# Down projections of two feed-forward layers as token rows, by seven block products in place of eight

## The reference, cut to what matters

```python
def squared_relu_mlp(h, w_up, w_down):          # (512, 1024), (1024, 4096), (4096, 1024)
    return jnp.square(jax.nn.relu(h @ w_up)) @ w_down

for i in range(DEPTH):                          # DEPTH = 2
    ...                                         # mixer and cross-attention
    h = h + squared_relu_mlp(rms_norm(h, norm_ffn[i]), ffn_w_up[i], ffn_w_down[i])
return rms_norm(h, norm_final)
```

## Time and profile before

| | |
|---|---|
| median of three runs | 1913.2 us |
| profiled execution, span | 1909.6 us |
| TensorE busy | 1857.5 us, 97% |
| VectorE busy | 1052.6 us, 55% |
| ScalarE busy | 747.2 us, 39% |
| GpSimd busy | 168.8 us, 9% |
| mean granted TensorE clock | 0.996 of full speed |

### The profile page before, as it was taken

One profiled execution on the slowest core, in us unless ns is written; L12 is line 12 of the kernel. 1 busy time (PEld: TensorE's weight loads), 2 busy tenths in 40 slices (PEclk: granted clock), 3 DMA queues, 4 the chain that ended last, 5 costly groups with the idle time before them and its releaser, 6 DMA issues.

```text
span 1909.6 us, 38661 instructions
## 1 busy us (share of the span) xinstructions
PE 1857.5 (97%) x17053; PEld 1527.4 (80%) x17053; DVE 1052.6 (55%) x1405; ACT 747.2 (39%) x999; POOL 168.8 (9%) x135
## 2 busy tenths in 40 slices
PE   6999999999999999999999999999999999999997
PEld 5898658778888888785779999998787788888886
DVE  4897655444432442447659888887654344324422
ACT  4434664334422332223544434343643343213322
POOL 1000002000000000210013111111020010000000
PEclk9999999999999999999999999999999999999999
DMA  6226223213332232453442112112362123332221
GB/s 215 89 71 233 78 100 133 66 45 93 106 111 88 89 111 88 137 159 127 154 147 62 51 50 53 49 31 70 126 217 70 44 89 102 97 110 89 88 88 44
DMA packets 165503, 189.41 MB, mean 99 GB/s; under 512 B 11801, under 2 KB 152646, under 8 KB 163674
## 3 DMA queue, kind: packets, MB, share of 16 engines
q1 hardware_dynamic: 162016, 174.44, 28.8%
q0 software_dynamic: 3088, 12.45, 1.7%
q10 hardware_dynamic: 234, 0.06, 0.0%
HBM read 161.22 MB, written 21.51 MB: 96 GB/s over the span
## 4 chain that ended last, share of the span: by engine, by line
PE 51%; DVE 3%; ACT 2%; issue 1%; DMA 1%; ACTq 0%; DVEq 0%
PE ps L357 11%; PE ps L358 10%; PE ps L359 10%; PE ps L2372 7%; PE ps L2338 2%; PE ps L2385 1%; PE ps L2326 1%; PE ps L1706 1%; PE ps L2349 1%; PE ps L1313 1%; PE ps L1746 1%; PE ps L2468 1%; ACT weights_split L326 1%; PE ps L2305 1%; PE ps L1294 1%
## 5 line engine op out<-in xcount | busy, mean ns | idle before, releaser
L344 DVE TENSOR_TENSOR weights_split<-w,weights_split 128x2048 fp32r<-128x2048 f32 x117 | 268.1, 2291 | 243.1 <-ACT weights_split L326 238.2
L326 ACT ACTIVATE weights_split<-w 128x2048 fp32r<-128x2048 f32 x118 | 225.9, 1914 | 285.7 <-PE ps L359 265.9
L357 PE MATMUL ps<-x_hn_hi,weights_split 128*128 128x512 f32 x640 | 252.7, 395 | 0.0
L359 PE MATMUL ps<-x_hn_hi,weights_split 128*128 128x512 f32 x640 | 249.2, 389 | 0.0
L358 PE MATMUL ps<-x_hn_lo,weights_split 128*128 128x512 f32 x640 | 249.0, 389 | 0.0
L357 PE MATMUL ps<-f_hidden_hi,weights_split 128*128 128x512 f32 x512 | 199.3, 389 | 0.0
L359 PE MATMUL ps<-f_hidden_hi,weights_split 128*128 128x512 f32 x512 | 199.2, 389 | 0.0
L358 PE MATMUL ps<-f_hidden_lo,weights_split 128*128 128x512 f32 x512 | 199.2, 389 | 0.0
L1565 DVE SCALAR_TENSOR_TENSOR f_relu<-ps,x_squares 128x512 f32<-128x512 f32 x64 | 44.1, 692 | 191.1 <-PE ps L359 172.5
L358 PEld LDWEIGHTS ps<-x_hn_lo,weights_split 128*128 128x128 f32 x640 | 120.2, 188 | 26.3 <-issue 1.4
L357 PEld LDWEIGHTS ps<-x_hn_hi,weights_split 128*128 128x128 f32 x640 | 120.1, 188 | 26.2 <-issue 1.4
(11 more groups left out here) (365 smaller groups left out, 3464.0 us busy)
## 6 DMA issues: line engine op xcount, KB each, us to landing
w<-in_ffn_w_up_dram SPq DMA_DIRECT2D x32, 1024.0 KB, 5.4
w<-in_ffn_w_down_dram SPq DMA_DIRECT2D x32, 1024.0 KB, 5.0
w<-in_xattn_w_kv_dram SPq DMA_DIRECT2D x15, 1024.0 KB, 5.4
w<-in_ab_w_in_dram SPq DMA_DIRECT2D x10, 1024.0 KB, 5.1
w<-in_xattn_w_q_dram SPq DMA_DIRECT2D x8, 1024.0 KB, 5.0
w<-in_xattn_w_o_dram SPq DMA_DIRECT2D x8, 1024.0 KB, 4.9
w<-in_ab_w_out_dram SPq DMA_DIRECT2D x4, 1024.0 KB, 5.5
w<-in_rwkv_w_r_dram SPq DMA_DIRECT2D x4, 1024.0 KB, 5.9
```

The costliest lines, as they stand in the source:

```text
L326: act.activation(hi, raw, ACT.Copy).then_inc(k.w_hi_ready, 1)
L344: eng.tensor_tensor(lo, raw, hi.bitcast(F32), ALU.subtract).then_inc(k.w_lo_ready, 1)
L357: pe.matmul(out, lhs[0], rhs[0], start=start, stop=False)
L359: return pe.matmul(out, lhs[1], rhs[0], start=False, stop=stop)
```

## The change

Only the down projections, the hidden chunks that they read, and what comes after them change; the products with `w_up` stay as they are.

**Seven products.** The 4096 hidden units go in four quarters of 1024. In a quarter the down projection is a product of a 2 x 2 block matrix of hidden values (token halves by halves of the hidden units) with a 2 x 2 block matrix of weights (512 rows by 512 columns). It is computed with seven block products in place of eight, each for 256 tokens by 512 output columns: P1, P2, P5, P6, P3, P7, P4 in this order, each 24 matmuls of 512 columns (4 chunks of rows, 2 token tiles, 3 of `mm3`). The hidden values are now the stationary operand, the weights the moving one, and outputs are token rows.

**Hidden blocks.** Two chunks (one slot of `w_up`) give seven 128 x 256 pieces for the seven products: four squares and three sums. `tm` holds eight pieces and is used once at a time. Of the first chunk, VectorE makes the relu (L1642), ScalarE squares it in place (L1523), VectorE subtracts (L1704), ScalarE rounds two pieces (L1526), VectorE takes their remainder (L1652); of the second chunk the same with three sums (L1708 to L1710, each waiting for the former), five pieces to be rounded and left over.

**Weight sums.** A quarter has 4 slots of `w_up` and 4 raw slots of `w_down`, and 11 splits: four, three raw blocks, and four sums. `combine` (VectorE, L397) makes a sum in place, a subtraction of 128 x 2048. A fourth weight buffer (`f_weights`) is added in the feed-forward.

**Output.** VectorE takes each product's two tiles from PSUM and adds them to the sums `down_sums_left` and `f_down_sums_right` (128 tokens x 512 each, L1664 to L1678). In layer 0 the sums are transposed back at the end, 32 transposes, and added to `h`, and only then are the eight chunks squared and the squares added on GpSimd. In layer 1 `h` is transposed into the sums during the first quarter (ScalarE copies them), and at the end each row tile is squared with its row sum on ScalarE, the root taken by Sqrt and reciprocal, and the rows scaled in place and stored.

The diff, cut to its core:

```diff
@@ weights, Kernel.plan_weights
-            for half in range(0, FF, FF // 2):
-                cols(f"up{l}", i["ffn_w_up"][l], half, half + FF // 2)
...
+            for r in range(0, FF, D):
+                cols(f"up{l}", i["ffn_w_up"][l], r, r + D)
+                rows = i["ffn_w_down"][l][r:r + D, :].rearrange("(j k p) c -> k p j c", k=2, p=P)
+                for b, n in ((0, 1), (1, 1), (0, 0), (1, 0)):
+                    self.slots.append((f"down{l}", [(None, None, rows[b, :, :, n * D // 2:(n + 1) * D // 2])]))
...
+                    x12, x22, x11, x21 = range(s - 3, s + 1)
+                    n = len(self.units)
+                    self.units += [(x11, 0), (x21, 0), (x11, sums + 1), (x11, sums + 3), (x22, 0), (x12, sums + 2),
+                                   (x21, sums + 4)]
+                    sums += 4
+                    for x in (x12, x22):
+                        self.release[x] = (self.w_lo_ready, n + 6)
+                    self.release[x11] = (self.w_sums, sums)
+                    self.release[x21] = (self.w_lo_ready, n + 7)
@@ Split
+    def combine(self, dve, i, a, b):
...
+        dve.wait_ge(k.w_lo_ready, k.rested)
...
+        dve.tensor_tensor(flat(s), flat(sa), flat(sb), ALU.subtract).then_inc(k.w_sums, 1)
@@ stage_layer, TensorE
+            def down(q):
+                for x, (name, part, bank, u, half, right) in enumerate(PRODUCTS):
+                    ws.wait(pe, WF + NS * q + 4 + u)
...
+                        if by_row and m == 0:
+                            pe.wait_ge(s_hlo, 2 * (y0 + 4 * q + j) + x + 1)
+                        mm = mm3(pe, outs[m], [h[:, j, part, m * P:(m + 1) * P] for h in hid],
+                                 ws.wide_pair(WF + NS * q + 4 + u, j), j == 0 and name in ("P1", "P2", "P5"), j == 3,
+                                 bank is not None)
...
+                for n, c in enumerate(TURN):
...
+                        m = pe.transpose(k.bank(turned[n])[:, t * P:(t + 1) * P],
+                                         sums[c // 4][:, t, c % 4 * P:(c % 4 + 1) * P], k.ident)
+                    m.then_inc(k.done(turned[n]), 1)
                 squares[2].sum(pe)
@@ stage_layer, ScalarE
+                    for m in range(2):
+                        k.wait_freed(act, up[q][2 * a + m])
+                        r = tm[:, 3 * m:3 * m + 2, :]
+                        act.activation(r, r, ACT.Square).then_inc(s_hsq, 1)
+                        act.wait_ge(s_hcomb, 2 * y + m + 1)
+                        b = slice(3, 8) if m else slice(1, 3)
+                        act.activation(hid[0][:, a, b.start - 1:b.stop - 1, :], tm[:, b, :], ACT.Copy).then_inc(s_hhi, 1)
...
+                    ws.round(act, WF + NS * q + a + 2)
+                for x in range(7):
+                    ws.round(act, WF + NS * q + 4 + x + 2)
@@ stage_layer, VectorE
+                    relu(q, a, 0)
+                    dve.wait_ge(s_hsq, 2 * y + 1)
+                    dve.tensor_tensor(tm[:, 2, :], tm[:, 1, :], tm[:, 0, :], ALU.subtract).then_inc(s_hcomb, 1)
+                    remainder(q, a, 0)
+                    relu(q, a, 1)
+                    dve.wait_ge(s_hsq, 2 * y + 2)
+                    k.dve.link(dve, dve.tensor_tensor(tm[:, 5, :], tm[:, 0, :], tm[:, 3, :], ALU.add))
+                    k.dve.link(dve, dve.tensor_tensor(tm[:, 6, :], tm[:, 5, :], tm[:, 1, :], ALU.subtract))
+                    dve.tensor_tensor(tm[:, 7, :], tm[:, 4, :], tm[:, 6, :], ALU.subtract).then_inc(s_hcomb, 1)
+                    ws.rest(dve, W + a + 2)
+                    remainder(q, a, 1)
+                    if a == 2:
+                        ws.combine(dve, U + 2, U + 5, U)
+                    elif a == 3:
+                        ws.combine(dve, U + 5, U + 4, U + 5)
+                for x in range(7):
+                    if last and q == 3 and x == 6:
+                        break
+                    take(q, x)
+                    ws.rest(dve, U + x + 2)
+                    if x == 0:
+                        ws.combine(dve, U + 3, U + 4, U + 2)
+                    elif x == 1:
+                        ws.combine(dve, U + 6, U + 1, U + 3)
+                    if last and q == 3 and x == 4:
+                        dve.wait_ge(s_out, 16)
+                        for t in (2, 3):
+                            mean(t, t + 1)
+                        for t in (2, 3):
+                            root(t, t + 3)
+                            scaled(t, 0)
+                            scaled(t, 1)
```

More of the change, by code:

```diff
@@ L296, in __init__ @@
         self.k, self.base = k, k.splits
-        assert k.to_split[self.base] == s0, "slots are split in order"
+        assert k.units[self.base][0] == s0, "slots are split in order"
         k.splits += len(ends)
@@ L424, in mm_chunks @@
             o, t = tok
[L425 removed]
+            m = pe.matmul(k.bank(n)[:, o:o + width], src[:, c, t:t + P], k.raw(slot)[:, c, col:col + width],
                           start=(c == 0), stop=(c == 7))
@@ L1361, in _ @@
+            for q in range(4):
+                for a in range(4):
+                    i = WF + NS * q + a
+                    if q == a == 0:
+                        mm3_first(pe, k, up[0][0], ws, b_pair.both, lambda c: hf.wait(pe, c), WF)
+                        squares[1].sum(pe)
+                    else:
                         ws.wait(pe, i)
                         for m in range(2):
-                            n = down[half] + 2 * a + m
-                            if d == 0:
-                                k.take(pe, n)
```

439 lines of the change are left out of this document (252 added, 187 removed).

## The result

| | before | after |
|---|---|---|
| median of 4 runs each, us | 1912.53 (1911.54 to 1913.42) | 2007.11 (2005.48 to 2008.23) |
| profiled span, us | 1909.6 | 2006.1 |
| mean granted TensorE clock | 0.996 | 0.969 |

The ratio is 1.0494, with a 95% interval of 1.0479 to 1.0509: the changed kernel is 4.9% slower. The forecast was 2005 us.

What follows compares the result with a forecast made beforehand. TensorE bounds the old kernel; the changed one was to wait on the serial VectorE and ScalarE chain. 39.6 + 44.0 + 10.4 - 1.8 = +92.2 us gives a span of 2001.8, plus 3.6: 2005 us, range 1980 to 2032.

Steps and rivals of the forecast that it cites:

- a slot's chain: Serial VectorE and ScalarE work per slot of w_up: 12.65 us, 14.86 with a weight sum, where TensorE needs 10.88; chance 82%.
- differences of 256: VectorE's subtractions for the hidden sums, not in the earlier trace: 0.42 us each, bounds 0.27 and 0.68.
- Hand-overs: Passing work between engines: 0.04 us each, eleven per slot; 0.10 each would give 2025 us, inside the main case.
- A quarter's waits: TensorE waits 1.4 us before P1, 2.7 before its last row chunk, 6.7 before P2, then 1.6, 1.2 and 0.3.
- the signs named: Expected in the changed profile: TensorE share some 91%, named waits, quarters of 95.5 us, over 8 us idle between layers.
- The clock: Rival: TensorE's half clock after the wait before P2 falls on the path, +14 us, 2019 us; chance 6%.
- The rival of late weights: At quarter changes, weight slots share bandwidth and the first lands 2 us late: +12 us, 2017 us; chance 6%.
- The end of layer 0: Last product to the next stage's matmuls: squares, six GpSimd adds, sum with ones 1.3, entry 1.0; +10.4 us.
- The end of layer 1: Tail after P4 shorter by 7 us, P4 waiting 5.2 us for P7's bank: net -1.8 us.
- The turned copies: In layer 1's first quarter ScalarE copies two transposed chunks per slot ahead of the rounding: +4.4 us.
- The stages between: From the stage after layer 0 to layer 1's first relu: forecast change 0.
- The time around the span: Median above the profiled span by 3.6 us, added to the forecast span of 2001.8 us.

Runs made afterwards that it cites:

- round_early: The changed kernel with ScalarE rounding the next slot's weights right behind the second chunk's square, ahead of the copy of 1280: 1931.35 us.
- remainder_first: The changed kernel with VectorE taking the remainder of 1280 before the next slot's split remainder, in place of behind it: 1968.2 us.
- clock_held: The changed kernel with 26 extra TensorE matmuls before the wait for P2's weights, to keep its clock up: 2007.81 us.
- sums_moved: The changed kernel with two weight sums moved, from slot 3 to behind P2 and from behind P2 to behind P5: 1998.53 us.
- scaling_later: The changed kernel with VectorE, in layer 1's last quarter, taking P7's tiles before scaling the first two row tiles: 2004.75 us.
- all_orders: The changed kernel with early rounding, moved sums, later scaling, and GpSimd adding only four squares after layer 0, TensorE summing the rest: 1908.07 us.

## Why the prediction was right

**The bound.** It said that TensorE would stop being the bound because a slot's chain on the two other engines lasts longer than TensorE's 10.88 us. The slots of 12.59 and 14.81 us show it, and round_early and remainder_first show that it is the order, not VectorE's load: the same instructions in two other orders ended at 10.87 (TensorE's own time; the chain there is 9.93) and 11.20 us a slot.

**The durations.** The two sizes that were not in the trace came out as the slope of the others said: differences of 256 in 0.42 to 0.43 (0.42), the remainder of 1280 in 1.48 (1.49), the copy of 1280 in 1.27 (1.27). Hand-overs: relu 565.92 + 0.68 to its square at 566.64 is 0.04. The value of the earlier trace rows was the right end of the bound and the 0.10 of the earlier trace rows the wrong one; had it been 0.10 at each of the eight changes of engine in a slot, 12.65 would have become 13.1. (The prediction counts eleven; the order of a slot has eight, and two waits of VectorE for itself.)

**A quarter's waits.** Forecast 1.4, 2.7 and 6.7; the trace has 0.83, 2.34 and 5.14. Add the 0.27 that goes unrecorded at each wait and they are 1.1, 2.6 and 5.4. The last is short by 1.3 because the six matmuls ahead of it ran at the half clock, 6 x 0.20 = 1.2 us longer, and P2's start is set by VectorE: 53.66 against 54.05. Behind P2 the forecast had waits of 1.6, 1.2 and 0.3 us; the trace has none before P5 and 0.1 to 0.2 before P6 and P3, because P2's slow matmuls filled the time. P6 started 13.8 us behind P2's start, where 13.9 was forecast. Of the signs named, two came out a little off: TensorE's share is 93% and not 91%, as slow matmuls count as busy, and its wait for GpSimd's adds 7.9 us and not over 8.

**The clock.** The prediction gave 6% to a loss on the path of 14 us, and held that P2's would be covered: 5.69 + 1.7 = 7.4 us against VectorE's 7.30. It was covered, as clock_held shows, but by another sum. P2 took 8.2 us, and P5's split was ready after 7.0; the 1.2 us between were hidden by the wait before P6, with 0.1 us to spare. That it held is in part luck, and in sums_moved it held no longer. In two places there was no cover, and the clock was in no term: the sum with ones at the end of layer 0 (1.9 us of its 3.8) and P4 at the end (7.5 for 5.44). Together 4.0 us; these are the step that failed, a term left out: both follow a wait that the prediction itself had worked out (over 8 us, and 5.2 us), and the earlier trace rows had shown what comes after one. I had carried that to P2 alone. Nor had the clock fallen only once in the kernel before: it is 0.50 from 235 to 238 us too, behind idle times of 0.41 and 0.80 us.

**The weights.** The rival of late weights has nothing for it. The slots of `w_up` landed later after their issue than before (medians 7.4 us into `w` and 8.7 into `f_weights`, 5.4 before), but in neither feed-forward did TensorE, VectorE or ScalarE wait for a transfer.

**The end of layer 0** was +12.4 for +10.4: the add chain right to 0.1 us, the sum with ones 2.5 over, of which 1.9 are the clock and 0.6 a term sized too low, and the entry to the next stage 0.5 in place of 1.0. **The end of layer 1** was forecast at -1.8 with P4's wait and the shorter tail; both were right to 0.3 us. P4's slow 2 us does not show in the layer's sum (+41.7 for +42.2) since two other sizes were off the other way, which is luck. The turned copies cost 3.9 and not 4.4: the first quarter took 93.1 us in layer 0 (457.88 to 550.98) and 97.0 in layer 1 (1614.17 to 1711.15). And before, layer 1 took 336.2 us from its first relu to its last product (1559.35 to 1895.56) against layer 0's 334.4, which I had taken as equal. 39.5 + 3.9 - 1.8 for the quarters, and for the end 5.35 + 2.06 - 7.3: 41.7.

**The stages between** were taken as unchanged; their gaps of "issue" grew by 3.1 us, and the stages by 3.0. The gaps were 11.8 in scaling_later's profile with the same instructions there, so part of this differs from execution to execution. What makes them stays open.

**The time around the span** was taken as 3.6 us, the median of before less the profiled span. The executions themselves show 1.8 us (2007.89 for a span of 2006.1), the rest was the distance between two executions. The forecast's 2005 thus came out 2.1 below 2007.11 with a span 4.3 below 2006.1; with the 1.8 it would have been 2003.6. A part of its closeness is luck.

**The expectations** were a little lower than the result, by 2 to 5 us, the largest in all_orders (1903 for 1908.07); only clock_held's range held the result. Each assumed that nothing but the named step would wait, and sums_moved's left out the clock.

## What to carry to other kernels

Before taking work off the engine that is the bound, add up for one stage of the loop the chain on the engines that feed it, with each one's order and with every tile that exists once, and compare it with the bound engine's new time for that stage; mean busy shares (55% and 39% here) say nothing on it. If the chain is longer, look for the in-order engine whose next independent instruction stands behind a wait: one such instruction moved ahead of its wait was worth 76 of 95 us. And wherever the sum has a long idle time of TensorE, ask whether what stands behind it is on the path, and then cost its first microseconds at the half clock. What hides that loss is often the same wait that one would like to remove: in sums_moved the second quarter gained nothing, since P2's slow matmuls came out from under it.

## What the runs showed of the hardware that was not expected

- The half clock came after shorter waits than the one of 4.42 us in the earlier trace rows. In the changed kernel the matmuls of 596.57 lie 0.43 us apart behind an idle time of 2.34 us, with one of 0.83 us at 589.86 ahead of it, and those behind the 0.83 alone lie 0.23 apart.
- The same idle times are not always followed by it. In sums_moved's fourth quarter waits of 0.83 and 2.33 us stand ahead of the matmuls of 784.88, and these lie 0.23 us apart at a granted clock of 1.00. And it can come late: behind 3.18 us of idle time the matmuls of the changed kernel from 469.21 on start at the full clock, and only from 470.63 on, over a microsecond later, do they lie 0.43 apart.
- P4's matmuls were slow for about 4 us behind 5.35 us of idle time (1991.88 to 1995.86), P2's for about 5.3 (604.64 to 609.93) behind 5.14, and in the last quarter for only 2.7 behind 5.69 (1955.68 to 1958.41).
- A square that also sums its row is followed by a read of the accumulator, an instruction of its own: the read starts 0.54 us behind the square, the next square 0.76.

```profile
1984.65 0.64 ACT L1550 ACTIVATE f_squared<-down_sums_left 128x512 f32<-128x512 f32 x1
1985.19 0.18 ACT L1550 ACTIVATION_READ_ACCUMULATOR f_squared<-down_sums_left 128x1 f32 x1
1985.41 0.63 ACT L1550 ACTIVATE f_squared<-down_sums_left 128x512 f32<-128x512 f32 x1
```
